# Two transformer-like blocks on one core: the memory norms' first wait, the place of input's first norm, and the order in which the second layer's last head is prepared

## The reference, cut to what matters

```python
def first_block(x, mem, mem_norm_w, norm_w, w_memkv, ...):
    mem_n = rmsnorm(mem, mem_norm_w)
    for i in range(DEPTH):
        h = rmsnorm(x, norm_w[i])
        ...
        mem_o = memory_attention(q_mem, mem_n, w_memkv[i])

# per head and chunk of the recurrence (second block), forward and reversed
bcum = cumsum(log_f)
o = (q * exp(bcum)) @ state + intra_chunk(q, k, v, bcum)
state = state * exp(bcum[-1]) + (k * exp(bcum[-1] - bcum)).T @ v
```

## Time and profile before

| | |
|---|---|
| median of 3 runs | 3240.36 us (3239.48 to 3247.62) |
| the profiled execution | 3237.17 us |
| its span | 3235.8 us |
| mean granted clock of TensorE | 0.956 |
| busy: TensorE, its weight loads | 2934.6 us (91%), 2402.1 us (74%) |
| busy: VectorE, ScalarE, GpSimd | 1628.1 (50%), 1041.0 (32%), 205.7 (6%) |

### The profile page before, as it was taken

How to read it: one execution, slowest core, us unless ns; L and a number is a source line. 1 busy time by engine, 2 the same in 40 slices (tenths; PEclk the granted TensorE clock), 3 DMA queues, 4 the chain that set the end, 5 groups by cost and what they waited for, 6 DMA issues and landing times.

```text
span 3235.8 us, 44928 instructions
## 1 busy us (share of the span) xinstructions
PE 2934.6 (91%) x18762; PEld 2402.1 (74%) x18762; DVE 1628.1 (50%) x3421; ACT 1041.0 (32%) x2010; POOL 205.7 (6%) x270
## 2 busy tenths in 40 slices
PE   7988899999999998888799999999899797799998
PEld 5767688888977566677568888888666686578886
DVE  3333545444445255677763433324825666654454
ACT  3223333223343245343242121212426344232222
POOL 0000000000000100100000000000211245100001
PEclk9999899999999999899899999999999798899999
DMA  6433322222222110222612212121120010223221
GB/s 219 139 126 134 109 75 59 59 59 59 72 85 104 52 33 1 82 79 79 205 43 91 66 52 73 46 78 66 40 60 20 21 37 14 92 91 99 96 93 63
DMA packets 227829, 248.75 MB, mean 77 GB/s; under 512 B 5568, under 2 KB 193068, under 8 KB 226092
## 3 DMA queue, kind: packets, MB, share of 16 engines
q1 hardware_dynamic: 227628, 245.89, 23.5%
HBM read 236.43 MB, written 9.44 MB: 76 GB/s over the span
## 4 chain that ended last, share of the span: by engine, by line
PE 55%; DVE 9%; ACT 4%; issue 2%; DMA 1%; POOL 0%; SPq 0%; ACTq 0%; DVEq 0%; POOLq 0%
PE PS L2155 52%; PE PS L2159 2%; PE PS L2364 1%; ACT AR L174 1%; DMA WR<-in_w_in 1%; DVE AR L2879 1%; DVE AR L3134 1%; ACT L169 1%; DVE STAT L3070 1%; ACT EX L174 0%; DVE AR L2894 0%; DVE EX L3121 0%; DVE AR L2890 0%; DMA WR<-in_w_mod 0%; ACT STAT L174 0%
## 5 line engine op out<-in xcount | busy, mean ns | idle before, releaser
L2155 PE MATMUL PS<-HI,WC 128*128 128x512 f32 (+2 forms) x1600 | 427.8, 353 | 0.6 <-DVE WC L3115 0.6
L2155 PE MATMUL PS<-AR 128*64 128x64 f32 (+8 forms) x3756 | 317.3, 268 | 66.3 <-ACT AR L174 24.6
L2155 PE MATMUL PS<-DW,DH 128*128 128x384 f32 (+1 forms) x1344 | 355.3, 346 | 1.0 <-ACT DH L174 1.0
L2155 PEld LDWEIGHTS PS<-AR 128*64 128x64 f32 (+5 forms) x3756 | 271.5, 171 | 113.0 <-issue 33.7
L174 ACT ACTIVATE AR<-PS 128x256 f32<-128x256 f32 (+4 forms) x389 | 165.8, 452 | 560.6 <-PE PS L2155 428.0
L2155 PEld LDWEIGHTS PS<-HI,WC 128*128 128x128 f32 x1600 | 283.9, 189 | 42.3 <-DVE WC L3115 1.1
L2155 PE MATMUL PS<-LO,WC 128*128 128x512 f32 (+2 forms) x800 | 282.2, 353 | 0.0
L2155 PE MATMUL PS<-HT,WR 128*128 128x256 f32 (+1 forms) x928 | 263.1, 437 | 20.7 <-ACT EX L174 6.2
L2155 PE MATMUL PS<-WR,HT 128*128 128x128 f32 (+2 forms) x1296 | 252.1, 352 | 12.5 <-ACT AR L174 5.4
L2155 PEld LDWEIGHTS PS<-DW,DH 128*128 128x128 f32 x1344 | 240.7, 191 | 9.7 <-issue 7.1
L2155 PEld LDWEIGHTS PS<-WR,HT 128*128 128x128 f32 x1296 | 192.0, 197 | 62.4 <-issue 41.0
(11 more groups left out here) (439 smaller groups left out, 4981.6 us busy)
## 6 DMA issues: line engine op xcount, KB each, us to landing
WR<-in_w_ffn_in SPq DMA_DIRECT2D x40, 1024.0 KB, 6.5
WR<-in_w_in_b SPq DMA_DIRECT2D x51, 512.0 KB, 6.1
WR<-in_w_mod SPq DMA_DIRECT2D x12, 2048.0 KB, 8.0
WR<-in_w_mod SPq DMA_DIRECT2D x24, 1024.0 KB, 5.4
WR<-in_w_ffn_out SPq DMA_DIRECT2D x22, 1024.0 KB, 4.9
WR<-in_w_in SPq DMA_DIRECT2D x40, 512.0 KB, 5.0
WR<-in_w_out SPq DMA_DIRECT2D x8, 2048.0 KB, 11.6
WR<-in_w_in SPq DMA_DIRECT2D x4, 2048.0 KB, 7.7
```

Source lines behind the costliest of these rows:

```text
L2155: mm = lambda o, l, r, start, stop: e.o.matmul(o, l, r, start=start, stop=stop, skip_group_check=True)
```

## The change

In the start, both memory norms' first steps are put ahead of `setup` and of the two weight pieces; they wait for the memory rows and the first constants alone. The constants' load counts on the semaphore `mem` now, so later waits on it are 16 higher. ScalarE's wait for all small loads is gone. TensorE's setup waits for `mem` too and uses bank 7. The norm2 steps of both memory blocks stand ahead of norm1 of input's first block. In layer 1 of the second block, head 3 gets a second KH buffer in HT's space, usable after the last projection, and its two directions are prepared in turns.

```diff
@@ class Ring
+    def add(self, ap, *points):
+        self.aps.append(ap)
+        self.until.append(points)
+        self.busy.append(False)
@@ build
+        items = [Norm(MX[:, i, :], [HT3], 512 + 128 * i, vec("mem_norm"), None, [("mem", 32)]) for i in range(2)]
+        for v in items:
+            norm_begin(v)
+        P.add("setup")
         fetch()
         fetch()
-        P.add("setup")
         P.add("inputs")
...
-        items = [Norm(MX[:, i, :], [HT3], 512 + 128 * i, vec("mem_norm"), None, [("mem", 16)]) for i in range(2)]
...
-        for v in items[:2]:
-            norm_begin(v)
         P.add("gz", [b["A"] for b in gbufs])
-        ths = [norm_end(items[0])]
+        ths = [norm_end(items[0]), norm_end(items[1])]
         norm_begin(items[2])
-        ths.append(norm_end(items[1]))
@@ prepare
-            for d, (k, lg, rev, order) in enumerate(H.dirs):
-                if d:
-                    yield
+            def direction(d):
                 jk, kh, kh_until = b["KH"].take()
...
+            if H.spare_keys is None:
+                for d in range(len(H.dirs)):
+                    if d:
+                        yield
+                    yield from direction(d)
+            else:
+                b["KH"].add(H.spare_keys, ("pj", P.count["pj1"]))
+                yield from rounds([direction(d) for d in range(len(H.dirs))])
             H.steps.sort()
@@ the layers of the second block
+            if not both:
+                heads[3].spare_keys = at(f"KH3{l}", HT_AT, 768, F32)
@@ TensorE
             def setup(n):
+                e.wait_ge("mem", 32)
                 e.wait_ge("const", CONST_N)
-                turn(bank(0), [VR[0:VTOT, :], BR_[0:96, :], GR[0:4, 0:96], GR[0:5, 128:256]]).then_inc(sem("set_pe"))
+                turn(bank(7), [VR[0:VTOT, :], BR_[0:96, :], GR[0:4, 0:96], GR[0:5, 128:256]]).then_inc(sem("set_pe"))
@@ ScalarE
-            def setup(n):
-                e.wait_ge("const", CONST_N)
-
@@ VectorE, setup
-                bk = bank(0)
+                bk = bank(7)
@@ SP
             def begin(n):
                 e.o.dma_start(MX, A["mem"].rearrange("o (i p) n -> p (o i) n", p=128)).then_inc(sem("mem"), 16)
-                for to, src in CONST_LOADS[:1]:
-                    e.o.dma_start(to, src).then_inc(sem("const"), 16)
+                e.o.dma_start(*CON_LOAD).then_inc(sem("mem"), 16)
 
             def setup(n):
-                for to, src in CONST_LOADS[1:]:
+                for to, src in CONST_LOADS:
                     e.o.dma_start(to, src).then_inc(sem("const"), 16)
```

More of the change, by code:

```diff
@@ L247, in __init__ @@
         self.state, self.q_ready, self.steps, self.lv, self.am, self.slots = {}, {}, [], {}, {}, {}
-        self.cum, self.kt, self.dec, self.begun, self.multiplied, self.ended, self.gneed, self.open_gate = {}, {}, {}, False, False, False, None, None
+        self.cum, self.kt, self.dec, self.begun, self.multiplied, self.ended, self.gneed, self.open_gate, self.spare_keys = {}, {}, {}, False, False, False, None, None, None
 def build(nc, A, out, dump=None):
@@ L1462, in build @@
         cols, cneed = scale_cols(CL[0:2], 0, 1, gcol(0, 0))
-        ctx_norms = [Norm(xt(i), [HT3], 128 * i, cols[1], modcol(0, 0, 1), [cneed, ("mem", 32)]) for i in (4, 5)]
+        ctx_norms = [Norm(xt(i), [HT3], 128 * i, cols[1], modcol(0, 0, 1), [cneed, ("mem", 48)]) for i in (4, 5)]
         for v in ctx_norms:
@@ L1541, in build @@
         FLOW = 0.64, 0.93
-        xneed = [("mem", 32)]
+        xneed = [("mem", 48)]
         def attention_stage(l, tiles, QKT, DV, BR, PAs, PTds, SQ, fill):
@@ L2664, in gt_end @@
                 e.activation(hi, v, ACT.Copy).then_inc(sem("gt_h"))
-            return dict(begin=begin, setup=setup, setup2=setup2, fence=fence, norm1=norm1, norm2=norm2, pj1=pj1, pjc=pjc, ma_x=ma_x, mod_h=mod_h, gs=gs, turn=turn_, gl=gl, hp1=hp1, hp3=hp3,
+            return dict(begin=begin, setup2=setup2, fence=fence, norm1=norm1, norm2=norm2, pj1=pj1, pjc=pjc, ma_x=ma_x, mod_h=mod_h, gs=gs, turn=turn_, gl=gl, hp1=hp1, hp3=hp3,
                         hl1=hl1, ho=ho, g1=g1, g3=g3, g6=g6, qturn=qturn, da_x=da_x, da_t=da_t, fnorm=fnorm, rr=rr, an=an, rs=rs, df_x=df_x, df_t=df_t, df_q=df_q,
@@ L3251, in build @@
         gw, sub = A["gla_norm_w"], A["da_subln_2"]
-        CONST_LOADS = [(CON[:, 0:136], A["k_const"][:, 0:136])]
-        CONST_LOADS += [(VR[VO[n_]:VO[n_] + w_, :], rows[n_]) for n_, w_ in VROWS]
+        CON_LOAD = CON[:, 0:136], A["k_const"][:, 0:136]
+        CONST_LOADS = [(VR[VO[n_]:VO[n_] + w_, :], rows[n_]) for n_, w_ in VROWS]
         CONST_LOADS += [(BR_[0:96, :], A["b_mod_2"].rearrange("l (a n) -> (l a) n", n=128)),
```

## The result

| | before | changed |
|---|---|---|
| median of 4 runs each | 3239.92 us (3239.35 to 3247.62) | 3223.89 us (3221.72 to 3226.86) |
| ratio | | 0.9947 [0.9935, 0.9959] |
| the profiled execution, its span | 3237.17, 3235.8 | 3226.86, 3225.6 |
| mean granted clock | 0.956 | 0.955 |

The forecast of 3226 and its range hold, and the change is faster by more than 0.3%. The profiled execution is the slowest of the four of the changed kernel, so its span shows 10.2 us of a gain whose median is 16.0. One execution of experiment 1 (3488.53 us at a granted clock of 0.82) was in a slower state of the chip; it counts in its median, not in its ratio.

The account below looks back on a forecast made before the run. TensorE was taken to bound the kernel, but not the two touched places. Start 8.0 plus last head 6.2 gives 14.2 off 3237.17, so 3223.0; the runs' median lies 3.2 higher, hence 3226 us, range 3218 to 3235.

Parts of the forecast that it names:

- Part 1: At the start: small loads ahead of weights and earlier memory norms ready the feature tile 8.7 to 7.3 us sooner, taken as 8.0.
- So the cover is thin but whole: At the start: input rows behind the weights still give a norm at 20.4 to 20.6, before TensorE wants it at 20.8.
- the first of its two ways: At the start: input rows, held behind the weight pieces, are issued at about 11.5 and land 6.6 us later, at 18.1.
- The sum by bytes: At the start: after a pause, 2.1 MB of weights and 1 MB of rows at 356 GB/s end at 17.9.
- Part 2: Last head of the second layer: second key buffer and new order save 4.5 us to the output, 6.2 in all.
- so this wait costs nothing: Last head: VectorE reaches the second buffer about when the last projection stops reading its space, at 2720.9, so no cost.
- TensorE's wait ahead of the output would fall under 6: Last head: a sign of success, TensorE's wait ahead of head 2's last output, 8.84 us before, ends under 6 us.
- The shared port: Last head: if VectorE and GpSimd exclude each other, three pairs take 4.6 each instead of 3.5, 3.2 us worse, near 3229.
- Rival 1: Start: the 3.29 us issue hold comes from the number of outstanding transfers, so the start gives 4.0; 3230 us, chance 0.14.
- Rival 2: Last head gives nothing, as VectorE reaches head 2's last mask no sooner; 3232 us, chance 0.14.
- Rival 3: Start: input rows take 12.0 us in the queue, TensorE stands 5 us, the start gives 3; 3231 us, chance 0.06.
- Rival 4: Start: every small load costs 3.29 us behind the memory transfer, making the kernel slower, 3266 us; chance 0.04.

Follow-up runs that it names:

- experiment 1: The changed kernel with only the start's edits, head 3 of layer 1 prepared as before; 3233.65 us, ratio 0.9977 against before.
- experiment 3: The changed kernel run again unaltered, for a second trace; 3225.44 us, ratio 0.9956 against before.
- experiment 2: The changed kernel with only the last head's edits, the start as before; 3234.02 us, ratio 0.9974 against before.
- experiment 11: The changed kernel run again unaltered on another chip, for a third trace; 3227.37 us, ratio 0.9953 against before.
- experiment 4: The changed kernel with the first half of input's rows issued between the two weight pieces, the second half behind them; 3225.75 us, ratio 0.9953 against before.
- experiment 10: The kernel of experiment 4 with the step `setup2` moved behind the second memory layer's first product; 3222.10 us, ratio 0.9938 against before.
- experiment 5: The changed kernel with the two weight pieces issued ahead of the small loads again; 3231.13 us, one execution.
- experiment 6: The changed kernel with input's first norm ahead of the second memory block's norm2 again; 3234.87 us, one execution.

## Why the prediction was right

**The sum.** 14.2 us were forecast. The fourth weight piece shows 7.9 for the start (8.2 and 6.3 in the other two traces), the stretch of the last head 6.3 (6.4 and 6.5). Experiment 3, the trace in which the clock took nothing between, ends 14.8 us ahead. On the medians the change gave 16.0, 16.0 and 14.1. The two places are less sharp than these figures look. For the start, 1.7 us of the 7.9 are the trace before having its half clock in the first product. For the last head, experiment 1 as the reference gives 5.0 and experiment 2 against before 8.0.

**Part 1.** Forecast 8.0, median 7.9. The steps before the first product were a little better than taken. The last small load is in at 8.6, since the weights stand behind it and not ahead of it; the first transposes start at 8.64 where 9.3 to 10.7 stood, and the first product is 9.1 us ahead, above the upper bound of 8.7. The step that failed is "So the cover is thin but whole: nothing lost, at most a few us if the rows are late." TensorE stopped before the input's norms, which the prediction had named as a sign of being wrong. The rows themselves landed nearly as said, at 18.36 against 18.1, but not by the first of its two ways: their issue starts at 8.25 and not at 11.5, and they take 10.7 us from issue to landing (median of the two halves) and not 6.6. The sum by bytes (17.9) is the one that held. But the moment at which TensorE wants them had been put at 20.8, from a start at 15.4 and a product of 5.4 us. It came at 18.15, from 14.46 and 3.69, and the wait was 2.76. Being early by more than planned was worth nothing, as a second transfer ends the stage: 14.60 and 5.38 in experiment 11 give the same second product within 0.3 us of experiment 3's 14.45 and 3.69. Two errors of opposite sign made 8.0 come true, which is luck. Experiments 4 and 10 show the size of the cover that was missing: 1.1 us beside experiment 11 (first product 5.3 to 5.4 us in both), 2.9 beside experiment 3 (3.69 in both).

**Part 2.** Forecast 6.2, measured 6.3. To the output: 4.5 forecast, 4.2 measured; VectorE's busy time was put at 27.8 and is 27.00, its idle time at 3.0 and is 4.15. Of the difference, 0.76 is the wait for the second buffer's space at 2717.47, of which the prediction said "so this wait costs nothing". Behind it: 1.5 to 2 forecast, 2.1 measured, with a wait of 3.17 for level products where VectorE had waited 4.27 for the last state products. Wrong was that TensorE's wait ahead of the output would fall under 6: it is 9.13 after 8.84. Its last products ahead of the output moved forward together with it, from an end at 2742.05 to one at 2733.97, so the wait keeps its length and comes earlier; TensorE's idle time in the stretch fell from 35.40 - 17.24 = 18.2 to 31.15 - 16.77 = 14.4 at other places, above all in its wait for direction 1's keys (6.20, now 1.89). A wait of the engine that isn't the bound was a poor sign to name.

**The shared port.** The Trainium skill, SBUF — State Buffer, section "Who interferes with whom", speaks of an exclusive lock between VectorE and GpSimd, which by the prediction's estimate would have cost 3.2 us here. The level products show less. Seven of VectorE and fourteen of GpSimd, begun together at 2734.7, are done 6.5 us later; alone they took 1.50 and twice 3.07, one after the other 7.6. In that time VectorE got through other operations as well. The long operations, seen one by one in the changed kernel, do show it:

```profile
2712.07 1.90 POOL L3189 TENSOR_TENSOR AR<-AR,WR 128x128 f32<-128x128 f32 x1
...
2724.71 2.54 POOL L3162 TENSOR_TENSOR AR<-EX,AR 128x768 f32<-128x768 f32 x1
...
2725.49 1.90 DVE L2889 TENSOR_TENSOR AR<-EX 128x128 f32<-128x128 f32 x1
```

The first is one GpSimd product, some 0.45 us alone, beside VectorE's scan from 2711.95 to 2713.72; another one beside the second scan takes 1.96. The last is one VectorE difference, 0.28 us alone, that ends at 2727.40, just behind GpSimd's long product at 2727.25. So the skill's rule agrees with the trace for the long operations and overstates the loss for the short ones. By an estimate from these rows 5.8 of VectorE's 27.00 us are such stretching: three lots of seven, 1.50 us each alone, take 4.34, 1.90 and 3.12, and a product of 0.96 takes 1.94. The 6.3 us stand as a measured sum; what the place would give without the shared port is not shown, but experiment 2, where VectorE's seven products were not stretched (1.49), reached the output 2.0 us sooner.

**The rivals.** Rival 1 fell by rows 1.73 and 7.18 of the changed kernel and by experiment 5: the next issues behind two weight pieces are held, whatever they are, and now these are the input rows' (2.28 for two). Rival 2 fell by experiment 2. Rival 3 appeared in a small form, 2.76 us instead of 5; its time in the queue (12.0) was nearly reached (10.7), but from an issue 3 us earlier. Rival 4 had its small loads at 3.29 us each and the turning point at 1.6; they take 0.29 to 0.61. What no forecast step priced by itself was experiment 6: the order of the norms alone decides over 4.7 to 6.6 of the 6.3 to 8.2 us.

## What to carry to other kernels

When a chain at the start is shortened, write down for each engine which transfer it wants next and when, at the earlier time and at the full clock: the next stop is there, and putting half of that transfer between the ones ahead of it removes it. An in-order queue punishes a step that was harmless as long as everything was late, so the order of steps has to be moved together with the loads. Judge gains of a few us by the stretch where they arise, in more than one trace, and not by the end of one trace or at a product far behind: the clock had moved two of the one-execution results here by 2.6 us before product 4000.

## What was not expected of the hardware

The granted clock differs between executions of one kernel, and mostly in the same few stretches (95 to 350, 1055 to 1170 and 1170 to 1485 us): the lead of the changed kernel over one trace of before ended at 10.3, 14.8 and 5.4 us, with 3225.6, 3221.0 and 3230.4 us of span. The last head's 6.3 to 6.5 us are in all three; with the new last head, nine traces have it at 64.8 to 65.3 us and experiment 2 at 63.27.

The first product of sixteen instructions took 3.69 us in two traces of the changed kernel and 5.38 in the third. There the granted clock around it (14 to 20 us) is 0.72. In experiments 1 and 4 it took 5.21 and 5.33 at a shown clock of 1.00. But the records of the clock begin in those traces only at 17.4 and 17.7 us, inside the product, so the 1.00 ahead of them may be a missing record; what slowed the product there is open. Over all thirteen traces it took 3.69 in five and 5.17 to 6.42 in eight.

An issue of a load is cheap or dear by what was issued ahead: 0.38 us behind the 1 MB of memory rows, 3.21 behind these and two weight pieces of 1 MB more. And the last of the small loads is there 1.5 us after its issue (7.1 to 8.6) when nothing large but the rows stands ahead, against 3.6 behind the weights.
